# The gated convolution of a hybrid decoder layer: units of projection ordered by channel block, with filter taps between the gatings

## The reference, cut to what matters

```python
def mix_inputs(x, pos, ln1, w_in):
    p = rmsnorm(x, ln1) @ w_in
    conv_in = p[..., :CONV_CH] * jax.nn.sigmoid(p[..., CONV_CH:2 * CONV_CH])
    # q, three sets of k and v (rotary on the first 16 of 64 columns), sigmoid gates: further columns of p
    ...
def conv_module(a_ext, dw_w, dw_b, ln_g, ln_b):
    y = lax.conv_general_dilated(a_ext, dw_w[:, None, :], window_strides=(1,), padding='VALID',
                                 dimension_numbers=('NWC', 'WIO', 'NWC'),
                                 feature_group_count=CONV_CH) + dw_b
    return jax.nn.silu(layernorm(y, ln_g, ln_b))
```

## Time and profile before

| what | us |
|---|---|
| median of three runs | 1816.92 (1816.48 to 1818.92) |
| the profiled execution | 1813.52 |
| its span, first to last instruction | 1811.8 |
| TensorE matmuls busy | 1439.0 (79%) |
| VectorE busy | 664.2 (37%) |
| ScalarE busy | 371.6 (21%) |
| GpSimd busy | 192.8 (11%) |

### The profile page before, as it was taken

One profiled execution on the slowest core, in us unless ns is written; L12 is line 12 of the kernel. 1 busy time (PEld: TensorE's weight loads), 2 busy tenths in 40 slices (PEclk: granted clock), 3 DMA queues, 4 the chain that ended last, 5 costly groups with the idle time before them and its releaser, 6 DMA issues. The chain is left out here.

```text
span 1811.8 us, 22638 instructions
## 1 busy us (share of the span) xinstructions
PE 1439.0 (79%) x7436; PEld 837.5 (46%) x7436; DVE 664.2 (37%) x1324; ACT 371.6 (21%) x794; POOL 192.8 (11%) x348
## 2 busy tenths in 40 slices
PE   5999999448569978873369990699999999999960
PEld 4665454148535555552235540354454454454430
DVE  3002999941137766653512228011011011011007
ACT  4000011013125555552111110011111111111113
POOL 0000011136110000002300000111111111111111
PEclk7999999769858999996679995799999999999985
DMA  8300000076142000004441100899999999999927
GB/s 319 137 1 6 12 15 18 14 271 190 53 121 71 1 1 1 1 17 130 128 166 49 67 29 2 324 412 412 412 406 413 414 403 413 412 401 409 407 94 285
DMA packets 79756, 336.98 MB, mean 186 GB/s; under 512 B 9770, under 2 KB 41643, under 8 KB 61698
## 3 DMA queue, kind: packets, MB, share of 16 engines
q1 hardware_dynamic: 61866, 287.76, 40.6%
q0 software_dynamic: 15440, 47.30, 7.6%
q10 hardware_dynamic: 2384, 1.06, 0.2%
HBM read 311.20 MB, written 29.45 MB: 188 GB/s over the span
## 5 line engine op out<-in xcount | busy, mean ns | idle before, releaser
L1630 PE MATMUL ps<-arena 128*128 128x512 f32 x544 | 241.1, 600 | 0.0
L1630 PEld LDWEIGHTS ps<-arena 128*128 128x128 f32 x544 | 102.6, 191 | 137.5 <-issue 137.4
L311 PE MATMUL ps<-arena 128*128 128x512 f32 (+3 forms) x432 | 159.0, 528 | 1.3 <-DVE arena L439 1.3
L453 DVE SCALAR_TENSOR_TENSOR arena<-arena 128x1024 f32<-128x1024 f32 x120 | 144.3, 1278 | 0.3
L1331 PE MATMUL ps<-arena 128*128 128x512 f32 (+1 forms) x288 | 129.5, 603 | 15.5 <-DVE arena L1426 15.5
L1684 PE MATMUL ps<-arena 128*128 128x512 f32 x272 | 121.6, 600 | 3.8 <-DMA arena<-scratch_h,ints 3.8
L1638 PE MATMUL ps<-arena 128*64 128x256 f32 x1088 | 121.2, 380 | 0.0
L277 PE MATMUL ps<-arena 128*128 128x352 f32 x384 | 116.1, 465 | 0.4 <-ACT arena L340 0.4
L311 PEld LDWEIGHTS ps<-arena 128*128 128x128 f32 (+1 forms) x432 | 77.3, 180 | 80.8 <-issue 73.7
L935 ACT ACTIVATE arena<-ps,arena 128x640 f32<-128x640 f32 (+7 forms) x128 | 89.9, 702 | 119.9 <-DVE arena L1010 108.5
L848 PE MATMUL ps<-arena 128*128 128x128 f32 x528 | 82.8, 287 | 35.6 <-ACT arena L945 32.0
(11 more groups left out here) (357 smaller groups left out, 1551.4 us busy)
## 6 DMA issues: line engine op xcount, KB each, us to landing
arena<-in_w_gate SPq DMA_DIRECT2D x34, 2048.0 KB, 11.4
arena<-in_w_up SPq DMA_DIRECT2D x34, 2048.0 KB, 16.0
arena<-in_w_down SPq DMA_DIRECT2D x34, 2048.0 KB, 16.1
arena<-in_x_prompt SPq DMA_DIRECT2D x16, 512.0 KB, 6.7
arena<-in_cache_cmp POOLq DMA_DIRECT2D x64, 128.0 KB, 3.2
arena<-in_cache_cmp SPq DMA_DIRECT2D x64, 128.0 KB, 2.7
arena<-in_cache_sel SPq DMA_DIRECT2D x64, 128.0 KB, 2.1
arena<-scratch_y SPq DMA_DIRECT2D x16, 512.0 KB, 5.9
```

Of the source, the lines that this page charges most:

```text
L311: mm = pe.matmul(ps[:n, b + o // 512, 0:w], xT[:, k, t * P:t * P + n], w_tm[:, k, o:o + w], start=(k == 0), stop=(k == KT_ - 1))
L453: ins = dve.scalar_tensor_tensor(o, i, dw[:, c, j:j + 1], o, ALU.mult, ALU.add)
L1630: mm = pe.matmul(ps[:, bank, :], xgT_l[:, k, :], w[LARGE][:, k, :], start=(k == 0), stop=(k == KT_ - 1))
```

## The change

- `w_conv` is loaded in two halves by channel block (blocks 0 and 1, then 2 and 3), each as two DMAs of 256 columns, the first half behind tile 2 and the second behind tile 5.
- TensorE turns tiles 0 to 2, projects a unit, turns two tiles, and so on for three units; from the fourth unit on all tiles are turned. ScalarE takes all squares before its first sigmoid.
- The units are ordered so that block 0 has its three pieces after unit 3 and block 1 after unit 5.
- Behind the gating of each unit from 3 on VectorE applies up to seven taps of blocks 0 and 1. Their results have places of their own, outside `w_conv`.
- The other taps, all of blocks 2 and 3, run in the tile loop, seven a tile.
- The wait of the tile projection for the last gating stands behind tile 0 instead of ahead of it.

```diff
+        acc_late = flat(A1 + KT_ * COLS_TM, 2 * TOKENS).rearrange("p (c n) -> p c n", c=2)
+        acc_prompt = [flat(AC, SEQ), gain[:, 0:SEQ], acc_late[:, 0, 0:SEQ], acc_late[:, 1, 0:SEQ]]
...
+        conv_order = [(0, 0), (0, 1), (1, 0), (2, 0), (1, 1), (2, 1), (0, 2), (1, 2), (2, 2), (0, 3), (1, 3), (2, 3)]
+        tiles_for = [-(-(j + 1) * NW // P) for j in range(3)]
+        block_done = [max(u for u in range(12) if conv_order[u][1] == c) + 1 for c in range(4)]
+        early_taps = [[] for _ in range(12)]
+        left = [[(c, j) for j in range(TAPS)] for c in range(2)]
+        for u in range(12):
+            for n in range(7):
+                ready = [c for c in range(2) if left[c] and u + 1 >= block_done[c]]
+                if ready:
+                    early_taps[u].append(left[ready[n % len(ready)]].pop(0))
+        late_taps = left[0] + left[1] + [(c, j) for j in range(TAPS) for c in (2, 3)]
+        tap_place = {what: n for n, what in enumerate([v for us in early_taps for v in us] + late_taps)}
...
+                def load_conv(half):
+                    for part in range(2):
+                        o = CH * part + 256 * half
+                        sp.dma_start(w_conv[:, :, o:o + 256],
+                                     a["w_in"].rearrange("(p k) n -> p k n", k=KT_)[:, :, o:o + 256])\
+                          .then_inc(sem(f"w_conv_in{half}"), 16)
...
+                    if t == 2:
+                        load_conv(0)
+                    if t == 5:
+                        load_conv(1)
...
-                for u in range(12):
-                    j, c = u // 4, u % 4
+
+                def project(u):
+                    j, c = conv_order[u]
+                    pe.wait_ge(sem("xT_act"), tiles_for[j])
+                    pe.wait_ge(sem("xT_dve"), tiles_for[j])
+                    pe.wait_ge(sem(f"w_conv_in{c // 2}"), 32)
...
+                for t in range(3):
+                    turn_x(t)
+                for u in range(3):
+                    project(u)
+                    turn_x(2 * u + 3)
+                    turn_x(2 * u + 4)
+                for u in range(3, 12):
+                    project(u)
                 pe.wait_ge(sem("w_tm_in"), 16)
-                pe.wait_ge(sem("glu_done"), 12)
...
+                    if t == 1:
+                        pe.wait_ge(sem("glu_done"), 12)
...
+                for t in range(TILES):
+                    moments(t)
+                    if 1 <= t <= 3:
+                        copy_x(t - 1)
+                for u in range(3):
+                    sigmoid(u)
+                    copy_x(2 * u + 3)
+                    copy_x(2 * u + 4)
+                for u in range(3, 12):
+                    sigmoid(u)
...
+                for t in range(5):
+                    normed(t)
+                    if 1 <= t <= 3:
+                        copy_x(t - 1)
+                dve.wait_ge(sem("dw_in"), 32)
+                dve.wait_ge(sem("pad_zero"), 1)
+                for u in range(12):
+                    glu(u)
+                    if u < 3:
+                        for t in (2 * u + 3, 2 * u + 4):
+                            copy_x(t)
+                            if t + 2 < TILES:
+                                normed(t + 2)
+                    for c, j in early_taps[u]:
+                        tap(c, j)
...
-                        dve.wait_ge(sem("tapped"), 4 * (j - 1) + c + 1)
+                        dve.wait_ge(sem("tapped"), tap_place[c, j - 1] + 1)
...
-                taps = [(c, j) for j in range(TAPS) for c in range(4)]
+                share = -(-len(late_taps) // TILES)
...
-                    for c, j in taps[14 * t:14 * t + 14]:
+                    for c, j in late_taps[share * t:share * t + share]:
```

More of the change, by code:

```diff
@@ L197, in build @@
         w_conv = flat(A1 + KT_ * COLS_TM, KT_ * D).rearrange("p (k n) -> p k n", k=KT_)
-        acc = flat(A1 + KT_ * COLS_TM, 4 * TOKENS).rearrange("p (c n) -> p c n", c=4)
+        acc_late = flat(A1 + KT_ * COLS_TM, 2 * TOKENS).rearrange("p (c n) -> p c n", c=2)
+        acc_prompt = [flat(AC, SEQ), gain[:, 0:SEQ], acc_late[:, 0, 0:SEQ], acc_late[:, 1, 0:SEQ]]
+        acc_sample = [flat(AC + SEQ + NB * NS * c, NB * NS) for c in range(2)] + \
+                     [acc_late[:, c, SEQ:TOKENS] for c in range(2)]
         tap_product = flat(A1 + KT_ * COLS_TM + 4 * TOKENS, TAPS * NB * NS).rearrange("p (j n) -> p j n", j=TAPS)
@@ L235, in _ @@
                         sp.dma_start(gain[:, 0:D], a["ln1"].partition_broadcast(P)).then_inc(sem("ln1_in"), 16)
-                sp.dma_start(w_conv, a["w_in"].rearrange("(p k) n -> p k n", k=KT_)[:, :, 0:D])\
-                  .then_inc(sem("w_conv_in"), 16)
+                    if t == 2:
+                        load_conv(0)
+                    if t == 5:
+                        load_conv(1)
                 sp.dma_start(dw, a["dw"].rearrange("p (c n) -> p c n", c=4)).then_inc(sem("dw_in"), 16)
@@ L255, in _, with turn_x @@
             def _(pe):
-                pe.wait_ge(sem("const_in"), 16)
-                for t in range(TILES):
+                def turn_x(t):
                     n = rows(t)
@@ L267, in _ @@
                     mm.then_inc(sem("x_turned"), 1)
-                pe.wait_ge(sem("xT_act"), TILES)
-                pe.wait_ge(sem("xT_dve"), TILES)
-                pe.wait_ge(sem("w_conv_in"), 16)
-                for u in range(12):
-                    j, c = u // 4, u % 4
+                def project(u):
[3 more added lines that the diff above has]
+                    pe.wait_ge(sem(f"w_conv_in{c // 2}"), 32)
                     if u >= 2:
@@ L280, in _ @@
                     mm.then_inc(sem("conv_projected"), 1)
+                pe.wait_ge(sem("const_in"), 16)
+                for t in range(3):
[6 more added lines that the diff above has]
+                    project(u)
                 pe.wait_ge(sem("w_tm_in"), 16)
-                pe.wait_ge(sem("glu_done"), 12)
                 def turn(t):
@@ L327, in _, with moments, copy_x, sigmoid @@
                 chain = Chain(act, sem("act_chain"), count["act"])
[L328 to L343, removed]
+                def moments(t):
+                    n = rows(t)
+                    act.wait_ge(sem(f"x_in{t}"), 16)
+                    chain(act.activation(p_sb[:n, 1, 0:D], x_all[:n, t, :], ACT.Square, scale=1 / 32,
+                                         accum_out=ms[:n, t:t + 1]))
+                    if t == 0:
+                        act.wait_ge(sem("const_in"), 16)
+                    act.activation(sd[:n, t:t + 1], ms[:n, t:t + 1], ACT.Sqrt,
+                                   bias=con("eps")[:n, 0:1]).then_inc(sem("sd_ready"), 1)
+                def copy_x(t):
+                    n, b = rows(t), 2 * (t % 2)
+                    act.wait_ge(sem("x_turned"), t + 1)
+                    act.activation(xT[:, 0:4, t * P:t * P + n],
+                                   ps[:, b, :].rearrange("p (k m) -> p k m", k=4)[:, :, 0:n],
+                                   ACT.Copy).then_inc(sem("xT_act"), 1)
+                def sigmoid(u):
                     act.wait_ge(sem("conv_projected"), u + 1)
@@ L414, in _, with normed, copy_x, glu @@
                 chain = Chain(dve, sem("dve_chain"), count["dve"])
[L415 to L433, removed]
+                def normed(t):
+                    n = rows(t)
+                    dve.wait_ge(sem("sd_ready"), t + 1)
+                    chain(dve.reciprocal(rstd[:n, t:t + 1], sd[:n, t:t + 1]))
+                    if t >= 2:
+                        dve.wait_ge(sem("x_turned"), t - 1)
+                    dve.scalar_tensor_tensor(xn[:n, t % 2, :], x_all[:n, t, :], rstd[:n, t:t + 1],
+                                             gain[:n, 0:D], ALU.mult, ALU.mult).then_inc(sem("xn_ready"), 1)
+                def copy_x(t):
+                    n, b = rows(t), 2 * (t % 2) + 1
+                    dve.wait_ge(sem("x_turned"), t + 1)
+                    dve.tensor_copy(xT[:, 4:8, t * P:t * P + n],
+                                    ps[:, b, :].rearrange("p (k m) -> p k m", k=4)[:, :, 0:n])\
+                       .then_inc(sem("xT_dve"), 1)
+                def glu(u):
+                    j, c = conv_order[u]
                     dve.wait_ge(sem("sig_ready"), u + 1)
@@ L442, in _ @@
                     gl.then_inc(sem("glu_done"), 1)
-                dve.wait_ge(sem("pad_zero"), 1)
-                dve.wait_ge(sem("glu_done"), 12)
                 def tap(c, j):
-                    o, i = acc[:, c, 0:SEQ], a_p[:, c, j:j + SEQ]
+                    o, i = acc_prompt[c], a_p[:, c, j:j + SEQ]
                     if j == 0:
+                        dve.wait_ge(sem("glu_done"), block_done[c])
                         ins = dve.tensor_scalar(o, i, dw[:, c, 0:1], dw[:, c, TAPS:TAPS + 1], ALU.mult, ALU.add)
                     else:
-                        dve.wait_ge(sem("tapped"), 4 * (j - 1) + c + 1)
```

(10 more changed lines are left out.)

## The result

| | before | the change |
|---|---|---|
| median of four runs | 1817.85 us (1816.48 to 1818.92) | 1791.18 us (1788.55 to 1792.68) |
| the profiled execution | 1813.52 | 1789.70 |
| its span | 1811.8 | 1788.1 |

The ratio is 0.9856 (95% interval 0.984 to 0.9873); the medians are 26.7 us apart. The forecast was 1791.0. The kernel before has a fourth timed run here, taken beside the change, so its median differs a little from the 1816.92 above.

A forecast was written before the change was run, and what follows sets the result against it. TensorE and VectorE carry about equal load, and the stage ends on VectorE, which began later. The next stage moves from 365.6 to 339.6, 26.0 us less: 1813.5 - 26.0 = 1787.5, plus 3.4 to the median, 1791.0; range 1785.5 to 1799.

The forecast's parts named there:

- VectorE was the one that came late: Tile projection stage: VectorE, idle earlier beside some 98 us of matmuls, reached tile 8's finished copies 13.5 us behind.
- Dependent taps cost 0.04 us each: Units 3, 4 and 9 to 11: a tap reading its predecessor's result takes 1.32 us, hand-over 0.04 included.
- The lateness forecast at 2 us in all: Units with early taps: VectorE falls behind TensorE by under 0.6 us a unit, 2 us in all.
- The cover of 8.4 us: Between units: VectorE may be 8.4 us late before TensorE, whose unit u waits for gating u-2, feels it.
- Rival (c): Units 3, 4, 9 and 10: dependent taps far longer; gain gone at 2.9 us, 1828 us total at 3.2; 3%.
- Unit 0 waits for tile 3, behind half of the weights in runs of 1 KB: Start: tile 3 lands at 19.4 at the full-queue rate; unit 0 starts at 23.3 instead of 35.87.
- Rival (a): Start: loads come late, at 206 GB/s; unit 0 starts at 27.2 and the time is 1795; 12%.
- The first unit and the turnings: Unit 0 to tile projection: first unit 12.0 us, twelve units 116.1, turnings 6.9; projection starts at 146.3 instead of 153.24.
- Rival (b): Between units: TensorE's clock falls at each group of turnings, three at 2.5 us, costing 7.5: 1798.5; 9%.
- The tile loop: Tile projection: TensorE's pace stays, tile 8's copies done 180.1 us behind the start, at 326.4; VectorE on time.
- The block's end: Behind tile 8: the output branch ends the stage at 339.0; next stage 0.58 us later, at 339.6 instead of 365.6.
- After it: Later stages: start from a barrier, load nothing ahead of it, so the gain of 26.0 us stays whole.

The follow-up runs named there:

- experiment 2: The change's early taps and unit order, but with the old start (one weight load behind x, all nine tiles turned first): 1791.3 us, ratio 0.9852.
- experiment 3: The change with up to ten taps behind each gating instead of seven, the same 62 in all: 1803.1 us, ratio 0.9935.
- Experiment 4: The change with tile 3 of x loaded ahead of the first half of the weights instead of behind it: 1786.5 us, ratio 0.9834.
- experiments 6: The change with the 62 late taps eight a tile over tiles 0 to 7, none behind tile 8: 1793.9 us, ratio 0.9875.
- 7: The change with the convolution's state taken behind tile 0 and late taps eight a tile, none behind tile 8: 1786.1 us, ratio 0.9836.
- experiment 1: The change's start without taps between gatings; all 124 stay in the tile loop, 14 a tile: 1807.3 us, ratio 0.9956.
- experiments 8: The change with tile 3 of x ahead of the weights, state taken behind tile 0, and late taps eight a tile: 1780.6 us, ratio 0.9805.
- 10: Repeat of the kernel with tile 3 ahead of the weights, state early and late taps eight a tile, beside the change: 1781.2 us, ratio 0.9804.

## Why the prediction was right

**VectorE was the one that came late.** Right, and the larger part: experiment 2 gives it 18 us. P to N is 194.3 to 195.0 in every profile with seven or ten taps behind the gatings and the block's end as in the change, against 212.2 to 212.3 without them.

**Dependent taps cost 0.04 us each.** Right, 1.32 us a tap. The lateness forecast at 2 us in all was 0.1, because each instruction starts a little before the one ahead has ended (78.72 + 0.53 = 79.25, first tap 79.16; 79.16 + 9.21 = 88.37, next start 88.28). The cover of 8.4 us was put to the test by experiment 3 and came out at 8.1. Rival (c) would have needed taps of 2.9 us.

**Unit 0 waits for tile 3, behind half of the weights in runs of 1 KB.** Right: the tile was there at 18.9 for 19.4, so the rate of a full queue was the right row (352 and 348 GB/s in the windows 12 to 14 and 14 to 16 us, while the weights came, for the row's 327), and unit 0 started at 22.56 for 23.3. Rival (a) would have had 27.2. The prediction's estimate from the 6.15 us for 1 MB of the Trainium skill (DMA: Bandwidth & Descriptors, "Bandwidth") had the tile at 25.3. The trace decides against that time here: 1024 KB at 350 GB/s are 3.0 us. Experiment 4 shows that the tile was what counted.

**The first unit and the turnings.** Right in kind, mis-sized by 1.3 us: 121.7 us from unit 0 to projection where 116.1 + 6.9 = 123.0 was said. The first unit took 11.4 us for 12.0 (the 12.0 ran to the sigmoid's start, 0.2 us behind the last matmul, and its low clock lasted a little longer), and three pairs of turnings 6.1 in all (121.7 less 11.4 and 11 x 9.47) for 6.9, since in a pair one takes 0.97 us. Rival (b) did not come: the units behind a pair took 9.63 and 9.71 us.

**The tile loop.** Right: 180.06 us to tile 8's copies for 180.1.

**The block's end.** The branch was the right one and it was mis-sized. From the last output DMA's issue the sum had 1.8 us to landing and 0.58 to the next stage, 2.4. The 0.58 is VectorE's distance, from the earlier trace rows, and GpSimd's is another: 339.24 - 335.08 = 4.16 us, and again 4.16 in experiments 6 (340.31 - 336.15) and 7 (334.28 - 330.12), landing included. This made the end 1.8 us later; with unit 0 0.7 earlier and the units 1.3 shorter it came out 0.4 us from the forecast, so that place was hit partly by errors that cancel.

**After it.** The gain was carried through to the end within the spread of executions. That 1791.0 met 1791.2 so closely is luck. The sum gave 1787.5 for the profiled execution, which took 1789.7, and then added 3.4 us, by which the median of the kernel before lay above its one profile. Those 3.4 us are spread and nothing that a kernel keeps: the median of the change lies 1.5 above its profile, and further profiles of the kernel before took 1820.6 and 1814.2.

## What to carry to other kernels

Where two engines carry the same load in one stage and one of them idles in the stage before, the time is in moving work forward, and how much fits is not the sum: it is how late each hand-over may be, one unit here, against how late the work makes it. At a block's end list every branch with its own way out, since the next-longest one is what you win down to, and take the distance from an engine's last work to the next stage from a row of that same engine. When two edits of an end give 2.5 us and nothing, try both together before dropping them.

## What the runs showed of the hardware

- From the end of GpSimd's last DMA issue to the next stage's first work 4.16 us passed, in three kernels, of which about 1.8 are the DMA's landing; from VectorE's last tap 0.58.
- The same program has its first unit at a clock that rises at different times. In the change the window 26 to 28 us has 0.98; in its repetition 0.86; in experiment 1, with the same start, 0.50:

```profile
26.00:28.00 2.00, 2.00 (x4) 1.01 (x3) 0.00 (x0) 0.00 (x0) 0.00 (x0) 0.50 1.07 389
```

  From unit 0 to projection that made 121.7, 121.9 and 123.0 us; the three profiles of the kernel before have 117.4, 117.7 and 116.5.

- In experiments 8 and 10 the transposes of tile 2 took 1.97 us where experiment 4, with the same start of the program, had 1.15. That this is the lower clock is read from their length alone: the window view has 1.00 there. Unit 0 started 1.0 and 0.9 us later than in experiment 4, but mostly for another reason: the constants came later, and ScalarE's first root could start at 9.55 and 9.43 instead of 8.71. Some 0.2 us are left for the slower transposes.

- Waits of 2.68, 2.07 and 2.12 us before a unit were followed by matmuls at a lower clock (11.40 us for 9.71; experiment 3), one of 2.10 was not. What decides is not shown.
